# fp32r scores, a shared copy and a new compressed stage in the prompt attention of a Hawk/NSA decoder

## The chip, the cores and the metric

The kernel runs on one core of a Trainium2 chip. The metric is the device time of one execution in microseconds. Engines are called by their short names: PE (TensorE), PEld (its weight loads), DVE (VectorE), ACT (ScalarE), POOL (GpSimd), SP (SyncE, which only issues DMAs here). PA, PB and PCD are regions of PSUM: PA and PB of three banks each, PCD of two.

## The reference, cut to what matters

One inference step of a two-layer trunk for a prompt of 1024 tokens and 8 samples of one token: a Hawk layer (RG-LRU), then a layer of native sparse attention (NSA), each with a ConvFFN. The attention has 16 heads of 64 dimensions in four groups of four; the 4 heads of a group share keys and values. The part that the change touches:

```python
def nsa_attend(q_rot, q_raw, gates, q_pos, ctx, kw, vw, kw_pos):
    ...
    s_c = jnp.einsum('bcgrd,bngd->bcgrn', qr, ctx['kc']).astype(jnp.float32) * scale
    m_c = (ctx['cend'][None, :] <= q_pos[:, None])[None, :, None, None, :]
    p_c = masked_softmax(s_c, m_c)
    o_c = jnp.einsum('bcgrn,bngd->bcgrd', p_c, ctx['vc'].astype(jnp.float32))
    ...
    imp = jnp.einsum('bcgrn,nj->bcgj', p_c, ctx['cmp_to_sel'])
    ...
    top_val, top_idx = lax.top_k(imp, n_top)          # 8 of 16 blocks of 64 keys
    ...
    s_s = jnp.einsum('bcgrd,bcgkd->bcgrk', qs, k_g).astype(jnp.float32) * scale
    p_s = masked_softmax(s_s, m_s)
    o_s = jnp.einsum('bcgrk,bcgkd->bcgrd', p_s, v_g.astype(jnp.float32))
    ...
    s_w = jnp.einsum('bcgrd,bkgd->bcgrk', qs, kw).astype(jnp.float32) * scale
    p_w = masked_softmax(s_w, m_w)                    # window of 512 keys
```

`ctx['kc']` and `ctx['vc']` are 63 compressed keys and values per group, each made by a two-layer MLP with GELU from 32 tokens. q_rot and the keys of the selected and window branch carry a rotation of the first 16 dimensions of a head; the compressed branch uses q_raw.

## The kernel before

Stages follow one another: up to 1566 us the Hawk layer, its ConvFFN, keys and values and the q product; 1566 to 1693 us the compressed stage; 1693 to 2065 us the attention of the selected and the window branch; then the sample attention, the out projection and the second ConvFFN. Dense products are three fp32r products, high x high, high x low and low x high (tile(), L2051), of 128x128 weights with 348 columns; SP streams the weights, POOL splits them.

**Attention.** The prompt is cut in blocks (r, t, i): head r of its group, t = 0 or 1 the pair of groups (their two heads lie in the row halves 0 to 63 and 64 to 127, half = 0 or 1), i a tile of 128 queries. There are 64 blocks of two units (branch b = 0 selected, b = 1 window), each with the key tiles of 128 up to the diagonal: 528 tiles in all, cut in 152 groups of up to four tiles (112 of 4, 8 of 3, 24 of 2, 8 of 1). Neighbouring tiles of one branch form a run (runs()), one matmul for each half. Step s of PE is written out by hand in att_pe: transposes of group s-5 (L1232), scores of group s (L1219), values of group s-6 (L1243). Scores are plain f32 products into PA (half 0) and PB (half 1). DVE (att_dve) takes them with a custom operation that adds a mask, scales, writes to the ring in SBUF and keeps the minimum (L1302 for selected tiles, L1305 for diagonal and window tiles); behind each the accumulator is read and DVE is drained. Before each half of a group it writes one element (memset, L1294). It also inverts the sums of a unit (L1319) and adds the finished block to oc (L1313). ACT does the exponentials of a unit (L1275) and copies the transposed probabilities of each group from PCD to pt (copy_out, L1268). POOL multiplies the probabilities by gate and inverted sum (L1346, L1350). PE may write scores g when both maxima of group g-2 are done (max_done), transposes g when the copy of group g-1 is done (pt_ready).

**Compressed stage.** compress_pe makes the hidden layer of compressed keys, then values (L915), ACT the GELU (L998), PE the second layer (L950, L954), DVE copies. Then 16 blocks u = (t, i), i the query tile, eight heads at once: PE scores (L964), DVE mask, maximum and difference (shifted(), L1072 to L1078), ACT exponential, DVE sum, reciprocal and product (L1091 to L1098) and the importance of the 16 selection blocks (L1101 to L1108), POOL the gate (L1337), PE transpose (L979), ACT copy, PE product with vc (L991), ACT copy to oc. After every fourth block the eight largest of 16 are found (select_four, L1036 to L1048). The stage also works through modulation products for later (L284, L291, L315), whose weights SP loads. q is rotated on the way: its 16 leading dimensions of each head were packed through DRAM (pack_out, pack_in), DVE multiplies and adds 2064 columns in three steps at u = 4, 5, 6 (L1127 to L1131), and ACT's queue writes them back in place (turned_out, turned_back); the attention's first score waits for them (q_back).

## Time and profile before

| | us |
|---|---|
| three executions | 3223.52, 3218.14, 3211.95 |
| their median | 3218.14 |
| profiled execution | 3215.75 |
| its span in the profile | 3214.0 |
| busy PE / DVE / ACT / POOL in the span | 3083.8 / 1953.8 / 858.4 / 1186.4 |
| compressed stage (1566 to 1693) | 127 |
| selected and window attention (1693 to 2065) | 372 |

Busy is time in which an engine has an instruction under way; for PE the ends are modelled, so its busy time is an upper reading. What a stage waits for is read in that stage alone.

### The profile page before, as it was taken

The numbers are of one execution on the slowest core, as the hardware profiler recorded it, in microseconds if no ns is written. First come the engines' busy times: TensorE is split into PE (matmuls) and PEld (weight loads), VectorE is DVE, ScalarE is ACT, GpSimd is POOL, SyncE is SP. The second block draws the span as 40 slices with busy tenths as digits, with TensorE's granted clock in tenths as the row PEclk, the third lists the DMA queues.
The fourth block names the chain that finished last, engine by engine and source line by source line (L and its number), as shares of the span: only waits on it lengthen the run. The fifth ranks groups of instructions, "written<-read, shape, count | busy, mean of one in ns | idle before, by whom it ended". The sixth has DMA issues, their size and how long they took to land.

```text
span 3214.0 us, 56523 instructions
## 1 busy us (share of the span) xinstructions
PE 3083.8 (96%) x22530; PEld 2823.5 (88%) x22530; DVE 1953.8 (61%) x3639; ACT 858.4 (27%) x1337; POOL 1186.4 (37%) x801
## 2 busy tenths in 40 slices
PE   6999999999999999999989999998999999999996
PEld 4898989999999999899856666676989999999996
DVE  4567277566574756856377777402178558585676
ACT  4555131100010101302137888502131101010011
POOL 1332424434444443234115656301424444444441
PEclk8999999999999999999979999999999999999998
DMA  5222332121221212321455000185221111111112
GB/s 205 72 81 76 145 117 86 66 73 66 77 82 53 75 47 96 125 78 60 138 204 198 2 3 2 62 260 179 106 91 47 47 47 47 46 46 46 46 47 116
DMA packets 78015, 277.90 MB, mean 86 GB/s; under 512 B 8858, under 2 KB 19362, under 8 KB 74546
## 3 DMA queue, kind: packets, MB, share of 16 engines
q1 hardware_dynamic: 75202, 256.83, 23.5%
q10 hardware_dynamic: 2576, 17.73, 1.6%
q8 instruction: 171, 2.80, 0.4%
q14 instruction: 66, 0.54, 0.1%
HBM read 247.54 MB, written 36.27 MB: 88 GB/s over the span
## 4 chain that ended last, share of the span: by engine, by line
PE 78%; issue 6%; DVE 5%; SPq 3%; ACT 3%; DVEq 2%; DMA 1%; POOL 1%; POOLq 1%; ACTq 0%
PE PB L2051 32%; PE PA L2051 30%; PE PA L1219 2%; PE PCD L1232 2%; SPq L1648 1%; SPq L1649 1%; PE PB L1243 1%; PE PA L1243 1%; PE PA L2087 1%; PE PB L2087 1%; DVE ring L1305 1%; ACT ring L1275 1%; ACT pt L1268 1%; PE PCD L284 1%; DMA mw<-in_mw 1%
## 5 line engine op out<-in xcount | busy, mean ns | idle before, releaser
L1822 POOL TENSOR_TENSOR w_hi<-w_raw,misc 128x1024 fp32r<-128x1024 f32 x192 | 377.4, 1966 | 1504.2 <-PE PA L2051 624.5
L1824 POOL TENSOR_TENSOR w_lo<-w_raw,w_hi 128x1024 fp32r<-128x1024 f32 x192 | 560.0, 2917 | 27.3
L2051 PE MATMUL PA<-hB_hi,w_hi 128*128 128x348 f32 x1272 | 273.6, 323 | 0.0
L2051 PE MATMUL PB<-hB_hi,w_hi 128*128 128x348 f32 x1272 | 272.3, 322 | 0.0
L2051 PE MATMUL PB<-hB_hi,w_lo 128*128 128x348 f32 x1272 | 271.5, 322 | 0.0
L2051 PE MATMUL PA<-hB_hi,w_lo 128*128 128x348 f32 x1272 | 271.5, 322 | 0.0
L2051 PE MATMUL PB<-hB_lo,w_hi 128*128 128x348 f32 x1272 | 271.0, 321 | 0.0
L2051 PE MATMUL PA<-hB_lo,w_hi 128*128 128x348 f32 x1272 | 270.8, 321 | 0.0
L2051 PEld LDWEIGHTS PB<-hB_hi,w_hi 128*128 128x128 f32 x1272 | 214.9, 188 | 0.4
L2051 PEld LDWEIGHTS PB<-hB_lo,w_hi 128*128 128x128 f32 x1272 | 215.1, 188 | 0.0
L2051 PEld LDWEIGHTS PA<-hB_lo,w_hi 128*128 128x128 f32 x1272 | 215.0, 188 | 0.0
L2051 PEld LDWEIGHTS PA<-hB_hi,w_hi 128*128 128x128 f32 x1272 | 214.1, 188 | 0.4
L2051 PEld LDWEIGHTS PA<-hB_hi,w_lo 128*128 128x128 f32 x1272 | 214.2, 188 | 0.0
L2051 PEld LDWEIGHTS PB<-hB_hi,w_lo 128*128 128x128 f32 x1272 | 214.1, 188 | 0.0
L1350 POOL TENSOR_SCALAR ring<-ring,gtok,psm 128x640 f32<-128x640 f32 (+7 forms) x256 | 196.3, 771 | 0.1
L1275 ACT ACTIVATE ring<-ring,nmx 128x640 f32<-128x640 f32 (+7 forms) x256 | 185.1, 728 | 7.8 <-DVE nmx L1305 7.3
L486 DVE TENSOR_TENSOR ua<-ua,rms 128x1032 f32<-128x1032 f32 x48 | 111.9, 2330 | 67.8 <-ACT ua L424 67.5
L1268 ACT ACTIVATE pt<-PCD 128x1024 f32<-128x1024 f32 (+3 forms) x152 | 137.2, 903 | 51.0 <-PE PCD L1232 51.0
L486 DVE TENSOR_TENSOR ub<-ub,rms 128x1032 f32<-128x1032 f32 x46 | 85.4, 1856 | 85.7 <-ACT ub L424 85.7
L374 DVE TENSOR_TENSOR t<-t,sq 128x1032 f32<-128x1032 f32 x28 | 48.7, 1738 | 139.8 <-ACT sq L368 138.5
L537 DVE TENSOR_TENSOR O<-O,PB 128x1032 f32<-128x1032 f32 x40 | 49.1, 1228 | 134.2 <-PE PB L2051 133.3
L424 ACT ACTIVATE ua<-PA 128x1044 f32<-128x1044 f32 x24 | 25.1, 1045 | 392.1 <-PE PA L2051 390.3
(616 smaller groups left out, 6688.6 us busy)
## 6 DMA issues: line engine op xcount, KB each, us to landing
w_raw<-in_w SPq DMA_DIRECT2D x196, 512.0 KB, 3.6
mt<-in_mw SPq DMA_DIRECT2D x32, 1024.0 KB, 5.0
pages<-in_pages SPq DMA_DIRECT2D x64, 384.0 KB, 4.2
x_dram<-X SPq DMA_DIRECT2D x12, 1032.0 KB, 4.2
X<-x_dram SPq DMA_DIRECT2D x3, 4128.0 KB, 13.5
mw<-in_mw SPq DMA_DIRECT2D x4, 2048.0 KB, 23.1
mt_even<-in_mw SPq DMA_DIRECT2D x8, 1024.0 KB, 5.2
mt_odd<-in_mw SPq DMA_DIRECT2D x8, 1024.0 KB, 5.6
```

The costliest lines, as they stand in the source:

```text
L486: dve.tensor_tensor(u[:, 2:2 + TOK], u[:, 2:2 + TOK], rms, ALU.mult)
L537: dve.tensor_tensor(dst, dst, ps, ALU.add).then_inc(sem("sum_out"), 1)
L1219: mm = pe.matmul(PS[half][:, g % 2, n * P:(n + w) * P], QR[hs, r + 4 * t, i * P:(i + 1) * P], KH[b][hs, t, k * P:(k + w) * P], start=True, ...
L1232: mm = pe.transpose(PCD[e][:, c:c + 64], ring[half][q, x * P:(x + 1) * P], ident[q, q])
L1243: mm = pe.matmul(PS[j % 2][64 * half:64 * half + 64, 2, 0:P], VT[b][:, k, t * P + 64 * half:t * P + 64 * half + 64], flat(pt[g % 2])[:, (h ...
L1268: act.activation(to, of, ACT.Copy).then_inc(sem("pt_ready"), 1)
L1275: act.activation(p, p, ACT.Exp, bias=nmx[:, u % 16, half:half + 1], scale=-1.0, accum_out=psm[:, u % 16, half:half + 1]).then_inc(sem("exp ...
L1350: pool.tensor_scalar(p, p, gtok[:, i, gate:gate + 1], psm[:, u % 16, half:half + 1], ALU.mult, ALU.mult).then_inc(sem("p_ready"), 1)
L1822: pool.tensor_tensor(hi, raw, zero.broadcast_to([P, 1024]), ALU.add)
L1824: pool.tensor_tensor(lo, raw, hi.bitcast(F32), ALU.subtract).then_inc(sem("w_split"), 1)
L2051: mm = pe.matmul(PS[ps][:, c, 0:width], w[:, w0:w0 + P], x[:, k, c * width:(c + 1) * width], start=(k == 0 and n == 0), stop=(k == K - 1 a ...
L2087: mm = pe.matmul(PS[(p0 + b) % 2][:, c, 0:CW], w[(t + b) % 2][:, k * P:(k + 1) * P], x[:, k, c * CW:(c + 1) * CW], start=(first and i == 0 ...
```

## The change

Five things are changed.

1. The scores of the attention become three fp32r products each, q_hi x k_hi, q_hi x k_lo, q_lo x k_hi. ACT writes k_hi (k_high, six parts: four at the end of the compressed stage, two for t = 1 in the middle of the attention), POOL writes k_lo (k_low) and, for every block, q_hi and q_lo (q_parts). Blocks now run with t outermost.
2. The copy of the transposed probabilities of groups g with g % 3 == 2 goes from ACT to DVE, ahead of DVE's maxima of the same step. These are 50 of 152 groups: 38 of four tiles, 3 of three, 7 of two, 2 of one. The memset stays before the first half of a group only.
3. The last of the four selections moves into the attention (rank_four at step 10, drop_four at steps 12 and 14).
4. The compressed stage: compress v is cut in parts of 8, 4 and 4 products between other steps, the GELU is done for keys and values apart with each table loaded ahead, the DVE steps of block u+1 are interleaved with those of block u, the importance sum is two additions for the larger tiles, selections are spread over two or three blocks, and 48 products on idle PCD banks (IDLE_C) stand before PE's wait for POOL.
5. q is rotated for t = 0 in the Q stage and for t = 1 at u = 1 to 3, 1032 columns at a time. SP loads the rotation tables and the packed q between the last weight tiles of Q. The attention no longer waits for the rows to be written back (POOL waits for them, by half), but for q and k parts.

```diff
     def stage_c_pe(pe):
...
         for u in range(16):
...
+            if u >= 2:
+                pe.wait_ge(sem("oc_done"), u - 1)
+            warm(pe, PCD[u % 2], IDLE_C[u])
             pe.wait_ge(sem("pg_ready"), u + 1)
...
     def stage_c_dve(dve):
...
-            if u + 1 < 16:
-                shifted(u + 1)
+            if more:
+                masked(u + 1)
             dve.wait_ge(sem("ce_ready"), u + 1)
...
             dve.tensor_reduce(C["cs"], s3, AXX, ALU.add)
             dve.drain()
+            if more:
+                highest(u + 1)
...
             dve.reciprocal(C["cs"], C["cs"])
             dve.drain()
+            if more:
+                lowered(u + 1)
             dve.tensor_tensor(s3, s3, bn(C["cs"], i), ALU.mult).then_inc(sem("pc_done"), 1)
             dve.drain()
...
-            if i % 4 == 3:
-                select_four(dve, t, i - 3)
-            if 4 <= u <= 6:
-                rotate_dve(dve, u - 4)
+            if 1 <= u <= 3:
+                rotate_dve(dve, u - 1, 1)
+            if u in (3, 7, 11):
+                rank_four(dve, t, i - 3)
+            if u % 4 < 2 and u >= 4:
+                drop_four(dve, (u - 4) // QT, (u - 4) % QT // 4 * 4, u % 4)
...
-    BLOCKS = [(r, t, i) for r in range(4) for t in range(2) for i in range(QT)]
+    BLOCKS = [(r, t, i) for t in range(2) for r in range(4) for i in range(QT)]
...
+    def k_high(act, part):
+        t, b, c0, c1 = K_PARTS[part]
+        act.activation(KHI[t, b][:, c0:c1], KH[b][:, t, c0:c1], ACT.Copy).then_inc(sem("k_hi"), 1)
+
+    def k_low(pool, part):
+        t, b, c0, c1 = K_PARTS[part]
+        pool.wait_ge(sem("k_hi"), part + 1)
+        pool.tensor_tensor(KLO[b][:, t, c0:c1], KH[b][:, t, c0:c1], KHI[t, b][:, c0:c1].bitcast(F32),
+                           ALU.subtract).then_inc(sem("k_split"), 1)
+
+    def q_parts(pool, j):
...
+        q = QR[:, r + 4 * t, i * P:(i + 1) * P]
+        pool.tensor_tensor(qhi[j % 3], q, zero.broadcast_to([P, P]), ALU.add)
+        pool.drain()
+        pool.tensor_tensor(QLO[:, r + 4 * t, i * P:(i + 1) * P], q, qhi[j % 3].bitcast(F32), ALU.subtract).then_inc(sem("q_split"), 1)
...
     def att_pe(pe):
...
-        pe.wait_ge(sem("q_back"), 16 * 4)
+        pe.wait_ge(sem("qpk_turned1"), 16)
...
             for b, k, x, n, w in runs(g, False):
-                for half in range(2):
-                    hs = slice(64 * half, 64 * half + 64)
-                    mm = pe.matmul(PS[half][:, g % 2, n * P:(n + w) * P], QR[hs, r + 4 * t, i * P:(i + 1) * P],
-                                   KH[b][hs, t, k * P:(k + w) * P], start=True, stop=True, skip_group_check=True)
+                ks = slice(k * P, (k + w) * P)
+                for m, (q, kk) in enumerate(((q_hi, KHI[t, b]), (q_hi, KLO[b][:, t, :]), (q_lo, KHI[t, b]))):
+                    for half in range(2):
+                        hs = slice(64 * half, 64 * half + 64)
+                        mm = pe.matmul(PS[half][:, g % 2, n * P:(n + w) * P], q[hs], kk[hs, ks], start=(m == 0), stop=(m == 2),
+                                       skip_group_check=True)
...
+    def by_vector(g):
+        return g % 3 == 2
...
     def att_act(act):
...
-            if 0 <= s - LAG:
+            if 0 <= s - LAG and not by_vector(s - LAG):
                 copy_out(s - LAG)
...
     def att_dve(dve):
...
                 if half == 0:
                     after(dve, sem("t_done"), EVICTED[g])
-                dve.memset(dmark, 0.0)
+                    dve.memset(dmark, 0.0)
...
+        def copy_out(g):
+            dve.wait_ge(sem("t_done"), g + 1)
+            after(dve, sem("pv_done"), g - 1)
+            to, of = both_rows(g)
+            dve.tensor_copy(to, of).then_inc(sem("pt_ready"), 1)
...
         for s in range(NG + LAG + 2):
+            if 0 <= s - LAG < NG and by_vector(s - LAG):
+                copy_out(s - LAG)
...
+            if s == 10:
+                rank_four(dve, 1, 4)
+            if s in (12, 14):
+                drop_four(dve, 1, 4, (s - 12) // 2)
...
-        stream(T_KV + 8, T_O)
+        stream(T_KV + 8, T_Q + 5)
+        tables_in(sp)
+        stream(T_Q + 5, T_Q + 7)
+        pack_out(sp, 0)
+        tile_load(T_Q + 7, (T_Q + 7) % 2)
+        pack_in(sp, 0)
+        tile_load(T_Q + 8, (T_Q + 8) % 2)
```

On PE, one step in the middle of the attention. Before, scores of a selected run of four tiles, values of the group before, transposes of the next:

```order
L1219 MATMUL PA<-k_sel,xq 128x512 [waits max_done]
L1219 MATMUL PB<-k_sel,xq 128x512
L1243 MATMUL PA<-pt_154,v_sel 64x128 [waits pt_ready,oc_added]
L1243 MATMUL PA<-pt_154,v_sel 64x128
L1243 MATMUL PA<-pt_154,v_win 64x128 x2
L1232 MATMUL PCD<-ident,ring_163 128x64 [waits pt_ready,p_ready]
L1232 MATMUL PCD<-ident,ring_163 128x64 x7
L1232 MATMUL PCD<-ident,ring_164 128x64 x8
L1219 MATMUL PA<-k_sel,xq 128x128 [waits max_done]
```

After, at such a place (line 1322 scores, 1346 values, 1335 transposes):

```order
L1322 MATMUL PA<-k_hi_190,q_hi_196 128x512 [waits max_done]
L1322 MATMUL PB<-k_hi_190,q_hi_196 128x512
L1322 MATMUL PA<-k_lo_194,q_hi_196 128x512
L1322 MATMUL PB<-k_lo_194,q_hi_196 128x512
L1322 MATMUL PA<-k_hi_190,q_lo 128x512
L1322 MATMUL PB<-k_hi_190,q_lo 128x512
L1346 MATMUL PB<-pt_154,v_win 64x128 [waits pt_ready]
L1346 MATMUL PB<-pt_154,v_win 64x128
L1335 MATMUL PCD<-ident,ring_165 128x64 [waits pt_ready,p_ready]
L1335 MATMUL PCD<-ident,ring_165 128x64 x7
L1335 MATMUL PCD<-ident,ring_166 128x64 x8
L1322 MATMUL PA<-k_hi_189,q_hi_197 128x512 [waits max_done,q_split]
```

One f32 product for each half becomes three fp32r products for each half, in turns between PA and PB; the steps around it stand as before.

On DVE, the steps of one group in the attention. Before (1294 memset, 1302 mask and minimum, 1319 reciprocal):

```order
L1319 RECIPROCAL psm<-psm 128x2 [waits exp_done]
L1294 MEMSET misc 1x1 [waits t_done,s_done]
L1302 ISA ring_163,nmx<-PA,selm 128x512
L1302 ISA nmx 128x1
L1294 MEMSET misc 1x1
L1302 ISA ring_164,nmx<-PB,selm 128x512
L1302 ISA nmx 128x1
L1319 RECIPROCAL psm<-psm 128x2 [waits exp_done]
```

After (1404 memset, 1412 mask and minimum, 1423 the copy, 1437 reciprocal, 1429 the addition to oc):

```order
L1429 TENSOR_TENSOR oc<-oc,PA 128x128 [waits pv_done]
L1404 MEMSET misc 1x1 [waits t_done,s_done]
L1412 ISA ring_165,nmx<-PA,selm 128x512
L1412 ISA nmx 128x1
L1412 ISA ring_166,nmx<-PB,selm 128x512
L1412 ISA nmx 128x1
L1423 COPY pt_155<-PCD 128x2x6x64 [waits pv_done,t_done]
L1437 RECIPROCAL psm<-psm 128x2 [waits exp_done]
L1404 MEMSET misc 1x1 [waits t_done,s_done]
L1412 ISA ring_165,nmx<-PA,selm,nmx 128x384
```

The second memset is gone, and in every third step a copy from PCD stands ahead of the next group's maxima and ahead of the reciprocal, with waits for the transposes and for the values that read pt last.

On DVE, one block of the compressed stage. Before, shifted() of the next block (first four rows), then this block's sum to importance, then a rotation step of 2064 columns:

```order
L1072 TENSOR_TENSOR PA<-PA,cadd 128x8x9 [waits pg_ready,sc_done]
L1074 TENSOR_REDUCE cm<-PA 128x8
L1076 TENSOR_TENSOR pbuf_165<-PA,cm 128x8x56
L1078 MEMSET misc 1x1
L1091 TENSOR_REDUCE cs<-pbuf_166 128x8 [waits ce_ready]
L1096 RECIPROCAL cs<-cs 128x8
L1098 TENSOR_TENSOR pbuf_166<-pbuf_166,cs 128x8x48
L1101 TENSOR_REDUCE im_178<-pbuf_166 128x2x48
L1106 TENSOR_REDUCE im<-im_178 128x2x16
L1108 TENSOR_TENSOR im<-im,im_178 128x2x15
L1129 TENSOR_TENSOR qsw<-qsw,sinT 128x2064
```

After (1103, 1106 and 1112 belong to the next block, 1136 to 1172 to this one):

```order
L1103 TENSOR_TENSOR PA<-PA,cadd 128x8x9 [waits sc_done]
L1136 TENSOR_REDUCE cs<-pbuf_168 128x8 [waits ce_ready]
L1106 TENSOR_REDUCE cm<-PA 128x8
L1143 RECIPROCAL cs<-cs 128x8
L1112 TENSOR_TENSOR pbuf_167<-PA,cm 128x8x56 [waits pg_ready]
L1147 TENSOR_TENSOR pbuf_168<-pbuf_168,cs 128x8x48
L1116 MEMSET misc 1x1
L1162 TENSOR_TENSOR imt<-pbuf_168 128x4x48
L1164 TENSOR_TENSOR im_188<-imt 128x2x48
L1170 TENSOR_REDUCE im<-im_188 128x2x16
L1172 TENSOR_TENSOR im<-im,im_188 128x2x15
```

The next block's steps now stand between this block's, the difference is taken four steps later, and the importance takes one step more.

## Rows read from the trace of the kernel before

**Rows 1.** Busy us of PE, PEld, DVE, ACT, POOL by stage, clock, DMA share, GB/s.
```profile
1566.00:1693.00 127.00, 104.30 (x700) 71.19 (x699) 80.20 (x296) 38.08 (x72) 12.81 (x20) 0.77 0.66 207
1693.00:2065.00 372.00, 357.16 (x5027) 244.11 (x5028) 275.44 (x1490) 314.73 (x665) 218.12 (x384) 0.98 0.11 40
```

**Rows 2.** Waits in the attention, 1693 to 2065: us in total, times, longest us.
```profile
DVE psm L1319 <- ACT ring L1275: 21.2, 38, 3.3
PE PCD L1232 <- ACT pt L1268: 8.5, 19, 0.8
PEld PCD L1232 <- POOL ring L1350: 8.0, 25, 0.5
DVE ring L1305 <- PE PCD L1232: 7.9, 7, 1.1
DVE oc L1313 <- PE PB L1243: 5.9, 1, 5.9
```

**Rows 3.** Timeline of DVE, one half of a group: start us, duration us, line, operation.
```profile
1952.81 0.06 DVE L1294 MEMSET misc<- 1x1 f32 x1 [0.18 <-issue]
...
1953.54 0.08 DVE L1305 DVE_READ_ACCUMULATOR2_ANT nmx<- 128x1 f32 x1
1953.73 0.06 DVE L1294 MEMSET misc<- 1x1 f32 x1
```

**Rows 4.** Accumulator reads of the maxima by line: ns min/median/max, first, last start.
```profile
L1305 DVE DVE_READ_ACCUMULATOR2_ANT nmx<- x336: 81/83/85, 1694.4 to 2054.1; 128x1 f32 x168
...
L1302 DVE DVE_READ_ACCUMULATOR2_ANT nmx<- x160: 80/83/85, 1696.2 to 2050.0; 128x1 f32 x160
```

**Rows 5.** Timeline of PE, passes of two score runs: start us, duration us.
```profile
1886.79 0.65 PE L1219 MATMUL PA<-k_sel,xq 64*128 64x512 f32 x1
1886.79 0.65 PE L1219 MATMUL PB<-k_sel,xq 64*128 64x512 f32 x1
1887.28 0.59 PE L1219 MATMUL PA<-k_sel,xq 64*128 64x512 f32 x1
...
1889.57 0.48 PE L1219 MATMUL PA<-k_win,xq 64*128 64x384 f32 x1
...
1889.90 0.48 PE L1219 MATMUL PA<-k_win,xq 64*128 64x384 f32 x1
```

**Rows 6.** Chain that ended last, dense Q product: start us, us, count.
```profile
1531.60 11.49 PE PA L2051 x72
```

**Rows 7.** Groups by form, POOL, compressed stage: busy us, mean ns.
```profile
L1337 POOL TENSOR_TENSOR pbuf<-pbuf,gtok 128x128 f32<-128x128 f32 x2 | 0.8, 402 | 0.3
```

**Rows 8.** Copies: ACT's in the attention (busy us, mean ns), DVE's (ns min/median/max).
```profile
L1268 ACT ACTIVATE pt<-PCD 128x1024 f32<-128x1024 f32 x112 | 113.7, 1015 | 37.9 <-PE PCD L1232 37.9
...
L780 DVE COPY v_win<-PCD x4: 680/686/692, 1475.4 to 1485.2; 128x512 f32<-128x512 f32 x4
...
L2359 DVE TENSOR_TENSOR t<-O,PB x8: 1212/1220/1222, 3190.8 to 3207.1; 128x1024 f32<-128x1024 f32 x8
...
L773 DVE COPY k_win<-kb x2: 694/695/696, 1439.7 to 1453.2; 128x1024 f32<-128x1024 f32 x2
```

**Rows 9.** Timeline of DVE, compressed stage: selection's ends, a rotation, an importance sum.
```profile
1608.94 0.29 DVE L1036 TENSOR_TENSOR im<-im,m 128x128 f32<-128x128 f32 x1
...
1611.92 0.23 DVE L1072 TENSOR_TENSOR PA<-PA,cadd 128x72 f32<-128x72 f32 x1
...
1616.38 2.31 DVE L1127 TENSOR_TENSOR qpk<-qpk,cosT 128x2064 f32<-128x2064 f32 x1
...
1638.51 1.04 DVE L1101 TENSOR_REDUCE im<-pbuf 128x128 f32<-128x512 f32 x1
```

**Rows 10.** Compressed stage at 1636 to 1654: its window, and DVE behind it.
```profile
1636.00:1654.00 18.00, 18.00 (x80) 11.66 (x79) 11.60 (x59) 4.74 (x11) 2.62 (x5) 0.50 0.50 175
...
1650.74 0.23 DVE L315 TENSOR_TENSOR modT<-PB,vec 128x72 f32<-128x72 f32 x1 [3.97 <-PE PB L291]
```

**Rows 11.** Timeline of PE at the head of the compressed stage.
```profile
1585.40 0.44 PE L950 MATMUL PA<-hid,w 128*64 128x126 f32 x4 [1.56 <-ACT hid L998]
```

More of the change, by code:

```diff
@@ L896, in q_dve @@
             dve.tensor_tensor(q[:, NPR:TOK], q[:, NPR:TOK], q[:, TOK + 1:TOK + NC], ALU.add).then_inc(sem("q_scaled"), 1)
+            if n == 5:
+                for step in range(3):
+                    rotate_dve(dve, step, 0)
         dve.drain()
@@ L906, in q_dve, with compress_pe @@
         dve.drain()
-    def compress_pe(pe, k2, ps):
-        for kv in range(2):
-            out = ps[kv][:, 0:260].rearrange("p (g c) -> p g c", c=65)
-            for m in range(16):
-                mm = pe.matmul(out[:, :, 1:65] if m < 8 else out[:, :, 0:64], C["w1k" if kv == 0 else "w1v"][:, m, :],
-                               k2(kv, m % 8), start=(m == 0), stop=(m == 15), skip_group_check=True)
+    def compress_pe(pe, kv, first, last):
+        out = PB[:, kv, 0:260].rearrange("p (g c) -> p g c", c=65)
+        for m in range(first, last):
+            mm = pe.matmul(out[:, :, 1:65] if m < 8 else out[:, :, 0:64], C["w1k" if kv == 0 else "w1v"][:, m, :],
+                           K2[kv][:, m % 8, :, :], start=(m == 0), stop=(m == 15), skip_group_check=True)
         return mm
@@ L969, in stage_c_pe @@
         scores(1)
+        compress_pe(pe, 1, 12, 16).then_inc(sem("cmp_mm"), 1)
         pe.wait_ge(sem("gates_ready"), 1)
+        pe.wait_ge(sem("cmp_hidden"), 3)
+        for half in range(2):
+            for t in range(2):
+                mm = pe.matmul(PB[64 * half:64 * half + 63, 2, t * 64:(t + 1) * 64], C["hid"][:, 1, 2 * t + half, 0:63],
+                               C["w2"][:, 1, :], start=True, stop=True, skip_group_check=True)
+        mm.then_inc(sem("cmp_mm"), 1)
         for u in range(16):
@@ L1097, in stage_c_dve @@
             dve.drain()
+            if more:
+                lowered(u + 1)
             dve.tensor_tensor(s3, s3, bn(C["cs"], i), ALU.mult).then_inc(sem("pc_done"), 1)
             dve.drain()
-            dve.tensor_reduce(C["im0"][:, :, 0:seen(i)],
-                              pb[:, 0:512].rearrange("p (r h n) -> p h n r", r=4, h=2)[:, :, 0:seen(i), :], AXX, ALU.add)
+            if more:
+                scores_read()
+            if u == 0:
+                dve.wait_ge(sem("cmp_mm"), 6)
+                for half in range(2):
+                    vs = slice(64 * half, 64 * half + 63)
+                    cp = dve.tensor_copy(C["vc"][vs, :, 64 * half:64 * half + 64],
+                                         PB[vs, 2, 0:128].rearrange("p (t n) -> p t n", n=64))
+                cp.then_inc(sem("cmp_ready"), 1)
+            by_row = pb[:, 0:512].rearrange("p (r h n) -> p r h n", r=4, h=2)[:, :, :, 0:seen(i)]
+            if i >= 4:
+                two = C["imt"][:, :, :, 0:seen(i)]
+                dve.tensor_tensor(two, by_row[:, 0:2], by_row[:, 2:4], ALU.add)
+                dve.drain()
+                dve.tensor_tensor(C["im0"][:, :, 0:seen(i)], two[:, 0], two[:, 1], ALU.add)
+            else:
+                dve.tensor_reduce(C["im0"][:, :, 0:seen(i)], by_row.rearrange("p r h n -> p h n r"), AXX, ALU.add)
             dve.drain()
             q4 = C["im0"].rearrange("p h (j q) -> p h j q", q=4)
-            im = C["im"][:, :, i % 4, :]
+            im = C["im"][:, i // 4, :, i % 4, :]
             dve.tensor_reduce(im, q4, AXX, ALU.add)
@@ L1283, in att_act @@
                     exps(u)
+            for n in range(2):
+                if s == LAST_GROUP[16 + 4 * n]:
+                    act.wait_ge(sem("s_done"), LAST_GROUP[8 * n + 7] + 1)
+                    k_high(act, 4 + n)
         act.drain()
@@ L1338, in stage_c_pool @@
                                gtok[:, i, t * 8:t * 8 + 8].unsqueeze(2).broadcast_to([P, 8, seen(i)]), ALU.mult).then_inc(sem("pg_ready"), 1)
+            if u == 12:
+                k_low(pool, 0)
+            if u in (13, 14):
+                q_parts(pool, u - 13)
+        k_low(pool, 1)
+        k_low(pool, 2)
+        q_parts(pool, 2)
+        k_low(pool, 3)
     def att_pool(pool):
+        split = 3
         for u in range(NU):
@@ L1344, in att_pool @@
             n = len(branch_tiles(i, b)) * P
+            while split < len(BLOCKS) and FIRST_GROUP[split] - 5 <= UNIT_END[u]:
+                q_parts(pool, split)
+                split += 1
+            if u in (34, 42):
+                k_low(pool, 4 + (u - 34) // 8)
             pool.wait_ge(sem("sum_inverted"), u + 1)
@@ L1639, in smp_sp @@
         sp.wait_ge(sem("oc_done"), 16)
-        sp.wait_ge(sem("q_back"), 16 * 4)
+        for t in range(2):
+            sp.wait_ge(sem(f"q_back{t}"), 32)
         sp.dma_start(ptab, a["page_table"]).then_inc(sem("ptab_in"), 16)
```

209 lines of the change are left out of this document (126 added, 83 removed).

## The prediction

> **What bounds the kernel now.** I read the stage windows first, then inside each touched stage the waits and a stretch of each engine's instructions. The dense stages (0 to 1566 us and 2065 to 3214 us) are not changed in their arithmetic, and PE is busy through them. What moves the time lies in two stretches: the compressed stage, 127 us, and the attention of selected and window branch, 372 us [rows 1].
>
> In the attention PE is busy 357 us of the 372, DVE 275, ACT 315, POOL 218 [rows 1]. That looks like a PE-bound stage, and its waits agree: PE and its loads wait 8.5 us for ACT's copies and 8 us for POOL, with some 10 us in smaller pieces, so PE's own need is about 345 us [rows 2]. But DVE's 275 us is not its need. After each of the accumulator reads there is a gap of 0.11 us (a read of 0.08 us from 1953.54, the next start at 1953.73) in which nothing else can start, since the code drains there [rows 3]. There are 336 + 160 = 496 reads [rows 4]. So DVE is held 275.4 + 496 x 0.11 = 330 us of 372. Its idle time is 42 us: 21.2 us waiting for ACT's exponentials, 7.9 us for transposes that free a ring slot, 5.9 us once at the very end, and 7 us in small pieces [rows 2]. DVE has 42 us of room, PE 27.
>
> **Part 1: scores as three fp32r products.** Today a run of scores is taken by each of two row halves side by side in two passes. A 512-column pass starts 0.49 us after the one before (1886.79, 1887.28), a 384-column pass 0.33 us (1889.57, 1889.90), so 0.86 to 0.96 ns per column and pass [rows 5]. A full-height fp32r product of 348 columns takes 11.49 / 72 = 0.160 us, 0.458 ns per column [rows 6]. Three of those instead of two passes save 2 x 0.86 - 3 x 0.458 = 0.35 ns, at the upper spacing 0.54 ns, and over 528 tiles of 128 columns (67,584) 23 to 37 us of PE. That holds if the two 64-row halves of an fp32r product also run side by side, which no row shows; if they run one after the other, six of 0.458 ns instead of two of 0.86 to 0.96 cost 55 to 70 us more. I take the saving, by the f32 halves that start together, and use 23. PE's need becomes about 322 us.
>
> The parts themselves: k_hi is four ACT copies at the end of the compressed stage, k_lo and the q parts are POOL's. A POOL operation over 128 columns takes 0.40 us [rows 7]; 64 blocks x 2 = 51 us on an engine with 154 us idle in the attention [rows 1], issued blocks ahead. Cost at the end: none; if POOL were late, the scores of a block would wait some 0.8 us. At the start, PE no longer waits for the rotated rows to come back, but for four k parts; I count these as equal.
>
> **Part 2: every third copy on DVE.** 50 of 152 groups leave ACT: 38 of four tiles, 3 of three, 7 of two, 2 of one. ACT needs 1.015 us for four tiles [rows 8]. DVE's price from PSUM is 0.686 us for 512 columns, and for 1024 columns, one operand in PSUM, 1.220 us; between SBUF and SBUF 1024 take only 0.695 us [rows 8]. Ends of such records lie some 0.07 us past the next start, so I take 1.15, 0.9, 0.63 and 0.36 us: 38 x 1.15 + 3 x 0.9 + 7 x 0.63 + 2 x 0.36 = 51.5 us. These go on DVE, in front of the maxima of the same step. (The Trainium skill, "VectorE: DVE Perf Modes", section "Why PSUM operands drop a tier", says that a PSUM operand holds fp32 to one element per cycle, since PSUM has one read port for DVE. The rows agree: 0.686 us for half the columns that take 0.695 in SBUF. By the SBUF row the term would be 29 us.)
>
> The second memset of each group goes: 152 x 0.06 = -9 us [rows 3]. The last selection moves in from the compressed stage: +3 us (1608.94 to 1611.92) [rows 9].
>
> DVE's need: 330 + 51.5 - 9 + 3 = 375.5 us, which alone is more than the 372 us of the whole stage. The bound passes from PE to DVE, and PE's 23 us do not reach the end. To the need come what DVE can't fill: 11 us at the start and the end (1.2 us until the first scores are there, 3.3 us for the last exponentials, 5.9 us for the last values [rows 2]) and inner waits. The inner waits were about 30 us (42 less 11); ACT has 50 copies less to do, so its exponentials come sooner, but a DVE copy now waits for transposes too, and I keep half, 15. Attention: 375.5 + 11 + 15 = 401.5, so **+29.5 us**. Bounds: no inner waits at all and 1.06 us per copy, 383, so +11; all 30 us of inner waits left, 416.5, so +44.5.
>
> **Part 3: the compressed stage.** One of its 16 blocks is a chain on DVE: masks, maximum, difference, sum, reciprocal, product, importance, each drained. What goes:
> - rotation of q, 3 x 2.31 us over both halves of the heads: half is now done in the Q stage, beside PE's products [rows 6]: -3.5 us by the row of the first step [rows 9].
> - the fourth selection, to the attention: -3 us [rows 9].
> - the importance sum, 1.04 us at 512 columns [rows 9], becomes two additions of some 0.35 + 0.25 us plus one gap, for the eight blocks with the most columns: -1.4 us by that.
> - the next block's scores are interleaved with this one's reciprocal and product, so some 3 drains of about 0.07 us fewer per block: -3 us.
>
> Further, DVE waits for PE in this stage; the largest piece is 3.97 us at 1650.74, right behind a stretch in which the granted clock was 0.50 (the lower level, 1.2 GHz) and PE was busy all 18 us [rows 10]. PE had waited much in the blocks before. The change issues 48 extra products on idle banks ahead of its waits, and rotates earlier, so that these waits shorten; I count -6 us, between 0 and -10. (That the clock stays high with it is not shown by any row.) At the head, compress v is cut up so that PE has work while ACT does its GELU: PE waited 1.56 us there [rows 11] and 1 us for the copies behind, and each table load of 1.28 us moves ahead: -2.5 us, between 0 and -4.4. At its end a 2.4 us wait for the rotated rows goes, but four k_hi copies and k_lo products stand in its place: 0 to -2.4.
>
> The sum, -3.5 - 3 - 1.4 - 3 - 6 - 2.5 = -19.4, and the parts are not all on the chain at once; I take **-18 us**, bounds -6 and -22. The moves on SP's queue (rotation tables and packed q ahead of the last Q weight tiles) pass two weight loads of 512 KB; the tile before takes over ten microseconds of PE, and I count nothing; a late tile would cost 2 or 3 us. The sample stage's load that now waits for a group of the attention is needed only after 2065 us: nothing.
>
> **Sum.** The profiled execution took 3215.75 us, 2.4 us below the median of the three. 3215.75 + 29.5 - 18 = 3227.25, and with one microsecond for the risk at the weight loads **3228 us**.
>
> **The rivals.**
> - *Copies are cheap, faster.* If DVE copies at near its SBUF speed (29 us) and no inner wait is left, attention is 330 + 29 - 9 + 3 + 11 = 364, -8 us, and with -18 the whole comes to 3190. For it: ACT had the copies on PE's path (8.5 us of waits), and PE's need falls. Against it: the 512-column row. A chance of 0.15. (The Trainium skill, "TensorEngine Tiling (Array Packing)", section "PSUM Bottleneck", advises to use both ScalarE and VectorE for taking results out of PSUM once TensorE is faster. By it the change is right; here VectorE has 42 us of room and is asked for 51.5.)
> - *Near balance.* Need as computed, but the inner waits vanish: 386.5 us, 3215.75 + 14.5 - 18 = 3212. Chance 0.10.
> - *The compressed stage keeps its slow clock.* The extra products then lengthen PE's blocks and only the shorter DVE chain counts, -6: 3215.75 + 30 - 6 = 3240. Chance 0.13.
> - *The score halves do not run side by side, or narrow fp32r products cost like f32 ones.* PE's need becomes 345 + 55 to 70 = 400 to 415, both engines are at the bound and wait for each other: attention +40 to +58 with 12 to 15 us of waits, the whole 3238 to 3256. It decides from 400 us of PE. Chance 0.12. This and the forecast end slower.
> - Forecast: DVE becomes the attention's bound, 3220 to 3236. Chance 0.50.
>
> Faster and slower go by 0.3%, 9.65 us, about what a measurement of this kernel can tell from no change: below 3206 and above 3225. Faster: 0.15 and 0.02 of the near balance. Same: 0.08 of that, and the lowest third of the forecast's own case, 0.17: 0.25. Slower: 0.33 + 0.13 + 0.12 = 0.58. The range takes in the near balance, the forecast, the slow clock and the split halves: 3208 to 3256.
>
> **What would show it.** In the profile after: DVE held (busy plus reads x 0.11) over 92% of the attention, its waits for PE and ACT small, PE waiting for maxima (the line of the scores waits for nmx) for tens of microseconds, where it was 8 before; the copy on DVE at 1.15 to 1.25 us mean; a score run of 512 columns in 3 x 0.235 us with both halves at the same start. The compressed stage 105 to 121 us, its clock above 0.9. I would be wrong if the copies take 0.7 us, if PE still is the one not waiting, or if the dense stages move by over 3 us.

## The result and the profile after

The changed kernel takes 3236.29 us, median of 5 executions (3232.26 to 3242.31), the kernel before 3217.47 us in the same count; the ratio is 1.0059 with a 95% interval of 1.0048 to 1.0071. It is slower by 18.8 us; forecast were 3228 us and a range of 3208 to 3256.

The profiled execution of after took 3242.31 us, the longest of the five, with a span of 3240.5 us. Its stages (columns as in [rows 1]; the second row shows the attention, from the first score at 1686.39 to the last addition to oc at 2089.56):

```profile
1562.80:1686.40 123.60, 110.97 (x796) 79.58 (x795) 74.56 (x277) 40.83 (x78) 16.82 (x27) 0.82 0.58 174
1686.40:2090.00 403.60, 349.36 (x5426) 277.77 (x5427) 318.49 (x1414) 282.48 (x618) 277.89 (x512) 0.98 0.12 40
```

From the first product of the compressed stage (1563.28) to the first score are 123.1 us, before 126.4. The attention takes 403.2 us, before 371.3. The stages behind take 1150.9 us, before 1149.7, and the part ahead 3.3 us less; both lie within what these two parts differ by over all profiles below (the part ahead ended between 1561.8 and 1567.3). Over all profiles a small gain ahead is left: the part ahead is the same in the eleven kernels with the code of after there, and ended at 1564.4 us on the mean; in the three with the code of before it ended at 1567.0. So -3.3 - 3.3 + 31.9 + 1.2 = +26.5 us between the two spans, and nearly all is the attention.

There PE waits for a new releaser, the copy on DVE. Its idle time (the stretch less its busy time) rises from 372 - 357.2 = 14.8 us [rows 1] to 403.6 - 349.4 = 54.2 us. Of the waits in the attention after (us in total, times, longest us), against [rows 2]; a row of PE and one of PEld can cover the same moments, so the two don't add up to idle time of PE:

```profile
ACT pt L1374 <- PE PCD L1335: 96.0, 69, 3.0
POOL misc L1482 <- DVE psm L1437: 95.1, 61, 4.3
...
PE PCD L1335 <- DVE pt L1423: 31.1, 34, 2.1
PEld PCD L1335 <- POOL ring L1486: 28.8, 49, 2.1
ACT ring L1381 <- DVE nmx L1415: 23.8, 39, 2.0
...
PE PCD L1335 <- POOL ring L1486: 11.2, 18, 1.9
...
PE PA L1322 <- DVE nmx L1415: 7.6, 10, 2.2
```

The last row is the wait of the scores for the maxima, which the forecast had put at tens of microseconds: it stayed at 8. The late maxima show one step on, in ACT's 23.8 us of waits for them before its exponentials (5.5 us in g1, with the copies taken back). ACT, relieved of 50 copies, now waits 96 us for transposes: time it was given and can't use. The copies themselves, all four forms (busy us, mean ns), against [rows 8]:

```profile
L1423 DVE COPY pt<-PCD 128x1024 f32<-128x1024 f32 x38 | 46.5, 1224 | 9.5 <-issue 4.5 <-PE PCD L1335 4.4 <-PE PB L1346 0.3
...
L1423 DVE COPY pt<-PCD 128x512 f32<-128x512 f32 x7 | 4.8, 692 | 1.1 <-issue 1.1
...
L1423 DVE COPY pt<-PCD 128x768 f32<-128x768 f32 x3 | 2.9, 957 | 0.5 <-issue 0.5
...
L1423 DVE COPY pt<-PCD 128x256 f32<-128x256 f32 x2 | 0.8, 424 | 0.3 <-issue 0.3
```

That is 55.0 us of busy time and, with the 0.07 us by which each such record runs past the next start, the 51.5 us of the forecast. A score run of 512 columns in three fp32r products, from a timeline of PE (start us, duration us), against [rows 5]:

```profile
1949.99 0.48 PE L1322 MATMUL PA<-k_hi,q_hi 64*128 64x512 f32 x1
1950.02 0.47 PE L1322 MATMUL PB<-k_hi,q_hi 64*128 64x512 f32 x1
1950.31 0.40 PE L1322 MATMUL PA<-k_lo,q_hi 64*128 64x512 f32 x1
1950.34 0.39 PE L1322 MATMUL PB<-k_lo,q_hi 64*128 64x512 f32 x1
1950.55 0.39 PE L1322 MATMUL PA<-k_hi,q_lo 64*128 64x512 f32 x1
...
1950.89 0.44 PE L1346 MATMUL PA<-pt,v_sel 128*64 128x128 f32 x4
```

Both row halves start 0.03 us apart, so they do run side by side. The three products take 0.32, 0.24 and 0.34 us up to the values behind, 0.90 us in all; two f32 passes took 1.01 us, from the first start in [rows 5] to the values behind them. These two runs are typical: over the runs of this size that nothing held up, the median is 0.89 us in after (69 runs) and 1.01 us before (71 runs). In the kernel before, the values behind start here:

```profile
1887.80 0.44 PE L1243 MATMUL PA<-pt,v_sel 128*64 128x128 f32 x4
```

### The profile page after: what moved, and what is told of

It is laid out like the page before. It is cut to its first block, busy times and chain, and to the rows that moved or that the text cites. A ratio compares the mean times of both kernels' runs of the same rounds, so it can differ in the third digit from the quotient of the medians.

```text
span 3240.5 us, 57584 instructions
## 1 busy us (share of the span) xinstructions
PE 3079.2 (95%) x23026; PEld 2862.5 (88%) x23026; DVE 1998.6 (62%) x3548; ACT 828.6 (26%) x1295; POOL 1250.7 (39%) x935
## 4 chain that ended last, share of the span: by engine, by line
PE 72%; DVE 8%; issue 7%; SPq 3%; POOL 3%; DVEq 2%; ACT 2%; POOLq 1%; DMA 1%; ACTq 0%
PE PB L2189 32%; PE PA L2189 30%; DVE ring L1415 2%; POOL ring L1486 2%; SPq L1785 1%; SPq L1786 1%; PE PA L2225 1%; PE PB L2225 1%; DVE ring L1412 1%; PE PCD L291 1%; DMA mw<-in_mw 1%; DVEq L1416 1%; POOLq L1488 1%; PE PCD L1335 0%; PE PB L1577 0%
## 5 line engine op out<-in xcount | busy, mean ns | idle before, releaser
L1381 ACT ACTIVATE ring<-ring,nmx 128x640 f32<-128x640 f32 (+7 forms) x256 | 185.5, 727 | 24.8 <-DVE nmx L1415 23.8
L1335 PEld LDWEIGHTS PCD<-ident,ring 64*128 64x128 f32 x2112 | 80.0, 139 | 76.1 <-issue 47.3
L1335 PE MATMUL PCD<-ident,ring 64*128 64x64 f32 x2112 | 99.0, 230 | 45.8 <-DVE pt L1423 31.1
```

What stands on the lines that cost most here:

```text
L1335: mm = pe.transpose(PCD[e][:, c:c + 64], ring[half][q, x * P:(x + 1) * P], ident[q, q])
L1381: act.activation(p, p, ACT.Exp, bias=nmx[:, u % 16, half:half + 1], scale=-1.0, accum_out=psm[:, u % 16, half:half + 1]).then_inc(sem("exp ...
```

## The experiments

Theory A is the one of the prediction: the copies load DVE beyond what the stage holds. B, C and the later letters stand in the expectations. The table has the length of the compressed stage (first product to first score) and of the attention (first score to last addition) in each profiled execution, and the median time of all executions with its ratio to the kernel before, run on the same chip. Each length comes from one execution. In the attention that is enough: four kernels whose attention is the same (g1, h1, h2, i4) took 372.7 to 373.5 us. In the compressed stage it is not: the same code took 112.2 to 123.1 us.

| kernel | compressed | attention | median us | ratio, 95% |
|---|---|---|---|---|
| before | 126.4 | 371.3 | 3217.5 | |
| after | 123.1 | 403.2 | 3236.3 | 1.0059 (1.0048 to 1.0071) |
| g1_copies_act | 116.2 | 373.4 | 3203.5 | 0.9958 (0.9941 to 0.9974) |
| g2_before_copies | 126.3 | 405.4 | 3252.2 | 1.0116 (1.0100 to 1.0133) |
| g3_f32_scores | 123.1 | 404.6 | 3244.2 | 1.0082 (1.0063 to 1.0101) |
| g4_f32_act | 116.2 | 378.2 | 3207.1 | 0.9972 (0.9962 to 0.9982) |
| h1_reduce | 115.5 | 372.7 | 3200.7 | 0.9937 (0.9924 to 0.9951) |
| h2_no_idle | 112.4 | 373.5 | 3207.1 | 0.9964 (0.9950 to 0.9977) |
| h3_lag6 | 112.9 | 362.6 | 3193.9 | 0.9930 (0.9917 to 0.9944) |
| h4_no_q_parts | 112.8 | 375.0 | 3208.6 | 0.9971 (0.9961 to 0.9982) |
| i1_lag6_reduce | 113.4 | 362.3 | 3191.4 | 0.9915 (0.9902 to 0.9929) |
| i2_before_lag6 | 129.7 | 365.3 | 3212.1 | 0.9979 (0.9970 to 0.9989) |
| i3_every_sixth | 112.2 | 389.1 | 3220.8 | 1.0011 (1.0001 to 1.0020) |
| i4_late_gate | 120.3 | 372.9 | 3212.5 (one) | |

### The copies: taken back, and put into the kernel before

g1 takes the copies back in the changed kernel:

```diff
     def by_vector(g):
-        return g % 3 == 2
+        return False
```

> The changed kernel with all copies of transposed probabilities back on ACT; fp32r scores, parts, new compressed stage stay. Theory A (the copies made DVE the bound of the attention): DVE's need falls from about 375 to about 324 us, the attention, 403 us in the profile after, comes to 355 to 370 us, and the time to 3193 to 3208 us, below both kernels. Theory B (the parts of q and k on POOL delay the gated probabilities, for which PE waited 40 us after and 10 us before): the attention stays at 390 us or more and the time at 3225 us or more.

g2 is the kernel before with only this put in (and ACT skips these groups):

```diff
         for s in range(NG + LAG + 2):
+            if 0 <= s - LAG < NG and (s - LAG) % 3 == 2:
+                copy_out(s - LAG)
```

> The kernel before with one edit: the copy of every third group moves from ACT to DVE. Theory A: DVE's need rises from 330 to 381 us, and with the waits that stay the attention takes 400 to 410 us (371 before); the time is 3246 to 3258 us. Theory B: the attention stays within 10 us of 371 and the time below 3228 us.

Both times came out in the range of theory A, and so did g2's attention; g1's attention lies 3.4 us above its range. Without the copies the attention falls by 29.8 us, to 373.4, and the kernel is 0.42% faster than before instead of 0.59% slower. With them alone (and with both memsets kept) the attention of the old kernel rises by 34.1 us, to 405.4. PE's wait for DVE's copy has the same size there as in after:

```profile
PE PCD L1232 <- DVE pt L1319: 32.0, 38, 2.0
```

Theory B falls: the attention did not stay at 390 us in g1.

### How far DVE could take copies: every sixth

```diff
     def by_vector(g):
-        return g % 3 == 2
+        return g % 6 == 2
```

> The changed kernel with every sixth group's copy on DVE, 25 in place of 50 (g1 has none). DVE's need becomes 324 + 26 = 350 us. Theory A with the waits seen in g1 and after (DVE idles 30 us when it is the bound, about 50 us when not): attention 376 to 384 us, time 3208 to 3216 us. Rival (DVE has room for half the copies): attention 373 us as in g1, time 3203 us.

Both readings miss, A by 5 us. 25 copies cost 389.1 - 373.4 = 15.7 us, the next 25 cost 403.2 - 389.1 = 14.1 us. There is no point up to which DVE takes copies for nothing, though its idle time in g1 is still 373.4 - 269.6 - 54.6 = 49 us. Nor does a copy cost its full 1.1 us: about 0.6 us each, from the first. Each 25 copies add 24 or 25 us to DVE's busy time (269.6, 293.8, 318.5) and take 8 to 11 us from its idle time (49, 41, 30); the rest makes the stage longer. PE's waits for the copy say the same, 15.8 us here and 31.1 us with twice as many:

```profile
PE PCD L1335 <- DVE pt L1423: 15.8, 14, 2.1
```

A copy on DVE stands in order between maxima of two groups. PE needs both, in turn: the maxima of group g-2 to write scores g, the copy of group g-1 to write transposes g. Moved to DVE, the copy comes later by what DVE is at, and the maxima behind it later by the copy. That this order, and not the sum of DVE's work, sets the price is how I read the even slope; no run moved the copy to another place in the step.

### The scores: f32 again, with and without the copies on DVE

```diff
             for b, k, x, n, w in runs(g, False):
                 ks = slice(k * P, (k + w) * P)
+                if j < 63:
+                    for half in range(2):
+                        hs = slice(64 * half, 64 * half + 64)
+                        mm = pe.matmul(PS[half][:, g % 2, n * P:(n + w) * P], q_hi[hs].bitcast(F32),
+                                       KHI[t, b][hs, ks].bitcast(F32), start=True, stop=True, skip_group_check=True)
+                    continue
```

> The changed kernel with each score run of all blocks but the last as one f32 product of the high parts (the low parts are made as before but not used, so the result is coarser). Theory A: PE has room, so 15 to 20 us more PE work add at most 8 us: attention 403 to 411 us, time 3236 to 3244 us. Rival C (PE's own path sets the attention in the changed kernel too): the whole 15 to 20 us show, 3251 us or more.

> Both edits: f32 scores of the high parts and all copies on ACT (low parts made, not used). What is left of the change is the new compressed stage, the parts on ACT and POOL, the single memset and the new order of blocks. Theory A: the attention is near the 371 us of before, 363 to 373, and the fp32r products are worth what this kernel lies above the one with only the copies moved back, 8 to 18 us; time 3205 to 3218 us. Theory B: attention 390 us or more.

With the copies on DVE the f32 scores change the attention by 1.4 us (403.2 to 404.6), though PE is busy 10 us more (349.4 to 359.4): rival C falls for the attention. The median time, 3244.2, is just above the range given, and 7.9 us above after; the profile shows no more than 5 us of that, and I leave the rest open. With the copies on ACT the fp32r products are worth 378.2 - 373.4 = 4.8 us, 3.7 us by the medians, whose intervals overlap. That is under the 8 to 18 expected, and far under the 23 to 37 us of PE that the prediction gave them. PE's busy time in the two (attention, columns as before):

```profile
1680.00:2058.20 378.20, 354.43 (x5032) 243.33 (x5032) 270.34 (x1363) 316.71 (x668) 278.25 (x512) 0.99 0.13 42
```

```profile
1679.00:2052.40 373.40, 343.59 (x5424) 272.88 (x5424) 269.60 (x1363) 317.78 (x668) 278.54 (x512) 0.99 0.13 43
```

354.4 against 343.6: PE saves 10.8 us, not 23. Of these less than half reach the end: PE's idle time is 373.4 - 343.6 = 29.8 us in g1 and 23.8 us in g4. The waits that grow are those for POOL, in g1

```profile
PEld PCD L1335 <- POOL ring L1486: 26.5, 42, 1.7
...
PE PCD L1335 <- POOL ring L1486: 14.1, 21, 1.4
```

and in g4 (the rows of PE and PEld overlap, so their sums, 40.6 and 21.4 us, say which wait grew and not by how much PE stands longer):

```profile
PEld PCD L1341 <- POOL ring L1492: 15.5, 38, 1.3
...
PE PCD L1341 <- POOL ring L1492: 5.9, 12, 1.1
```

g4 shows one thing more. Its attention was expected at 363 to 373 us and took 378.2, 6.9 us more than before, though it has the f32 scores and the copies where they were. So the rest of the change (parts of k and q, the new order of blocks, the selection moved in, one memset less) lengthens the attention: 371.3 + 6.9 - 4.8 + 29.8 = 403.2. No run takes these pieces apart but for the q parts, which follow.

### POOL's parts and the distance to the transposes

h4 is g4 without q parts:

```diff
         q = QR[:, r + 4 * t, i * P:(i + 1) * P]
+        if j < 63:
+            pool.drain()
+            pool.tensor_tensor(pmark, zero[0:1], zero[0:1], ALU.add).then_inc(sem("q_split"), 1)
+            pool.drain()
+            return
...
-                        mm = pe.matmul(PS[half][:, g % 2, n * P:(n + w) * P], q_hi[hs].bitcast(F32),
+                        mm = pe.matmul(PS[half][:, g % 2, n * P:(n + w) * P], QR[hs, r + 4 * t, i * P:(i + 1) * P],
```

> As g4 (f32 scores, all copies on ACT), and scores read q itself, so that POOL makes no q parts but for the last block (k high parts alone are used, the result is coarser). Theory G: POOL loses 50 us, PE's waits for it fall to about the 10 us of before, and the attention from 378 to 366 to 371 us, time 3196 to 3203 us. Rival H: the attention stays at 375 to 380 us.

The attention is 3.2 us shorter in the profile, the median 1.5 us higher. The two rows of waits for POOL go from 21.4 to 15.3 us. So 53 us of q parts on POOL cost 0 to 3 us with f32 scores; 375.0 us is the lower end of what rival H gave. h3 keeps them and gives the chain more room:

```diff
-    LAG = 5
+    LAG = 6
```

> As g1, with transposes six groups behind the scores instead of five. Theory G (with the q parts on POOL the gated probabilities come late: PE waits 40 us for POOL in g1, 10 us before, and this eats what the fp32r scores save): with one more step of slack these waits fall under 15 us, the attention from 373 to 355 to 365 us, time 3190 to 3196 us. Rival H (POOL is only the last of several waits; DVE, held about 324 us plus its own waits, sets the pace): the attention stays at 368 us or more.

The attention falls by 10.8 us to 362.6, the time by 9.5 us, both as theory G has it. The waits for POOL fall from 26.5 and 14.1 us to 13.6 us of PEld and none of PE:

```profile
PE PCD L1335 <- ACT pt L1374: 14.0, 35, 0.8
...
DVE psm L1437 <- ACT ring L1381: 13.6, 26, 3.1
PEld PCD L1335 <- POOL ring L1486: 13.6, 41, 0.9
```

Is this the change's doing, or does the loop gain from it anyway? i2 is the same edit in the kernel before:

> The kernel before with transposes six groups behind the scores. Theory G (the sixth group pays since POOL makes the q parts now; before, PE waited only 10 us for POOL): 0 to -5 us, 3212 to 3218 us. Rival I (a sixth group of slack helps any version of this loop): the attention falls by 8 us or more, from 371 to 363 or less, time 3209 us or less.

It gains 6.0 us there (3218.07 to 3212.05, both of this comparison), and 6.0 in the attention, between what theory G (up to 5) and rival I (8 or more) gave. So 6 of h3's 10 to 11 us come from a slack that the loop lacked before already. The other 4 to 5 belong to the changed loop. That they come from its late probabilities fits the shorter waits for POOL, but is not shown by itself: no run had six groups of lag with f32 scores, or without q parts.

### The compressed stage: importance sum and idle products

```diff
-            if i >= 4:
+            if False:
                 two = C["imt"][:, :, :, 0:seen(i)]
```

> All copies on ACT (as g1, 3203.5 us) and the importance sum again as one reduction in place of two additions. In the profile after the first addition took 0.86 to 1.31 us, and ended each time some 0.1 to 0.2 us behind POOL's gate product that started beside it; the reductions of before took 0.71 to 1.05 us. Theory D (the additions cost time, not save it): the compressed stage is 2 to 4 us shorter at the same clock, time 3198 to 3202 us. Rival (they are beside the chain): no change, 3203.5.

DVE's busy time in the stage falls from 74.6 to 70.8 us, the stage from 116.2 to 115.5, the median by 2.8 us; the intervals of the two overlap. Theory D had asked for 2 to 4 us in the stage, so only its direction and the median bear it out. The first addition (busy us, mean ns; g1) and the reductions of the same blocks (h1):

```profile
L1162 DVE TENSOR_TENSOR imt<-pbuf 128x256 f32<-128x256 f32 x2 | 2.6, 1292 | 0.1
...
L1162 DVE TENSOR_TENSOR imt<-pbuf 128x160 f32<-128x160 f32 x2 | 1.7, 858 | 0.0
...
L1164 DVE TENSOR_TENSOR im<-imt 128x128 f32<-128x128 f32 x2 | 0.6, 294 | 0.1
```

```profile
L1166 DVE TENSOR_REDUCE im<-pbuf 128x128 f32<-128x512 f32 x2 | 2.1, 1049 | 0.1
...
L1166 DVE TENSOR_REDUCE im<-pbuf 128x80 f32<-128x320 f32 x2 | 1.4, 719 | 0.0
```

Why does an addition of 256 columns take 1.29 us? Each starts beside POOL's gate product, which the product ahead of it on DVE has released, and ends behind it. One such pair in after, 160 columns on DVE, 320 on POOL:

```profile
1608.47 0.72 POOL L1459 TENSOR_TENSOR pbuf<-pbuf,gtok 128x320 f32<-128x320 f32 x1 [6.07 <-DVE pbuf L1147]
```

```profile
1608.52 0.86 DVE L1162 TENSOR_TENSOR imt<-pbuf 128x160 f32<-128x160 f32 x1
```

i4 is g1 with POOL released after the additions instead, where there are additions:

```diff
-            dve.tensor_tensor(s3, s3, bn(C["cs"], i), ALU.mult).then_inc(sem("pc_done"), 1)
+            dve.tensor_tensor(s3, s3, bn(C["cs"], i), ALU.mult)
+            if i < 4:
+                dve.drain()
+                dve.memset(dmark, 0.0).then_inc(sem("pc_done"), 1)
...
-                dve.tensor_tensor(C["im0"][:, :, 0:seen(i)], two[:, 0], two[:, 1], ALU.add)
+                dve.tensor_tensor(C["im0"][:, :, 0:seen(i)], two[:, 0], two[:, 1], ALU.add).then_inc(sem("pc_done"), 1)
```

> As g1, but for i of 4 and more POOL is told to start its gate product only after the two importance additions. Theory D (an addition of two SBUF operands is held up by POOL's product beside it): the first addition takes 0.3 to 0.45 us for 160 to 256 columns, where it took 0.86 to 1.31. Rival (its access pattern is slow by itself): the same 0.86 to 1.31 us.

```profile
L1165 DVE TENSOR_TENSOR imt<-pbuf 128x256 f32<-128x256 f32 x2 | 0.9, 426 | 0.1
...
L1165 DVE TENSOR_TENSOR imt<-pbuf 128x160 f32<-128x160 f32 x2 | 0.7, 326 | 0.0
```

The same additions take 0.43 and 0.33 us: POOL beside them is what held them up. (The stage took 120.3 us in the one profile of i4, 116.2 in g1. POOL's product and what follows it start later there, but the same code of the stage differs by more than that between profiles, so nothing is shown by it.) The profile of after has the other case as well, a product of 384 columns on DVE that meets a k_lo part on POOL and takes 1.08 us, where it took 0.56 in the kernel before and 0.55 in after's other product of this size, with POOL idle (a row each of POOL and DVE after, then the one of before):

```profile
1665.04 1.26 POOL L1287 TENSOR_TENSOR k_lo<-k_win,k_hi 128x512 fp32r<-128x512 f32 x1 [6.03 <-ACT k_hi L1282]
```

```profile
1665.64 1.08 DVE L1147 TENSOR_TENSOR pbuf<-pbuf,cs 128x384 f32<-128x384 f32 x1
```

```profile
1623.09 0.56 DVE L1098 TENSOR_TENSOR pbuf<-pbuf,cs 128x384 f32<-128x384 f32 x1
```

(The Trainium skill, "SBUF — State Buffer", section "SBUF: two separate sides", says that a DVE operation with two SBUF inputs and a POOL operation that reads SBUF lock each other out for a whole instruction. The traces agree: 1.29 us beside POOL, 0.43 us alone. A reduction has one input; in h1 each of the eight largest started within 0.05 us of POOL's product and ended within 0.05 us of it, after 1.05 us for 512 columns, so it ran beside it and did not wait for its end.)

h2 is g1 with the idle products left out:

```diff
-    IDLE_C = (4, 0, 0, 0, 12, 3, 0, 2, 8, 0, 0, 0, 12, 3, 2, 2)
+    IDLE_C = (0,) * 16
```

> As g1, without the 48 extra products on idle banks. Theory E (they keep the clock up in some stretches, but lie in PE's own chain where the clock is low: 16 of them took 3.75 us from 1637.62 at block 8): the compressed stage changes by less than 5 us in all, 113 to 120 us. Rival F (they hold the clock and are what the new stage gains): without them the compressed stage takes 122 us or more, time 3210 us or more.

The compressed stage of its profile is the shortest but one, 112.4 us, at a granted clock of 0.89, the median is 3.6 us above g1 and the intervals overlap: 48 products neither help nor hurt beyond what can be measured. The profiled execution was the fastest of h2's five, 3198.5 us against a median of 3207.1, so its stage may be shorter than is usual. Rival F is out for the profile; a loss of up to 4 us in the median stays possible.

### Both together

> All copies on ACT, transposes six groups behind, importance sum as one reduction: the sum of h3 and h1. If what they gain adds, 2 to 4 us less than h3's 3193.9, so 3188 to 3192 us; attention 360 to 365 us. If the reduction's gain is lost in the clock's course through the compressed stage, 3194 us.

i1 takes 3191.4 us, 0.85% less than before (0.71 to 0.98) and 1.4% less than after: the best kernel of the study. It is 2.6 us below h3, as h1 is 2.8 below g1; twice the same small gain, each within the intervals, so the reduction's part is likely and not shown.

## Why the prediction was right, and where it was not

**Result.** Direction and range held; +18.8 us against +12. Too small a gain in the compressed stage (the step that failed, below) made the difference; the attention came out within 2 us, in part by luck.

**DVE's need in the attention: right.** Forecast 375.5 us; measured 318.5 + 496 x 0.11 = 373.1 us. Its idle time, forecast as 11 + 15, is 30.1 us. The attention: 401.5 forecast, 403.2 measured, +31.9 against +29.5. That "DVE becomes the attention's bound" as the cause of the slowdown is borne out by g1 and g2, which move it by 30 and 34 us with the copies alone. "The bound passes from PE to DVE, and PE's 23 us do not reach the end": g3 confirms the second half, 1.4 us. The first half is too simple. If a bound had passed, the first 25 copies would have cost less than the next; i3 shows 15.7 and 14.1 us. The 42 us of room that I gave DVE [rows 2] are not room: more than half of a copy's time shows from the first one. A need plus waits that stay is no model for this loop either: DVE's idle time is 49, 41 and 30 us with 0, 25 and 50 copies. That it was near the 26 us of the sum at 50 copies, and that the 6.9 us of the rest of the change (g4) were not in the sum at all, is why I call the close number luck in part.

**The signs.** Of those that were named, four came: DVE held 373.1 of 403.2 us, 92.5%; its waits for ACT's exponentials 5.1 us in all, 21.2 before [rows 2]; the copy at 1.224 us; both halves at one start. PE's wait for maxima, said to grow from 8 to tens of microseconds, did not grow (7.6 us); PE waits 31.1 us for the copy itself, which must be done before its next transposes. The compressed stage, said to take 105 to 121 us at a clock above 0.9, took 123.1 at 0.82 in this profile, 112.2 to 116.2 at 0.90 to 0.94 in five others. And the part ahead moved by 3.3 us, just over the 3 that were to count against the forecast, which did not foresee it.

**fp32r products: the mechanism right, the term mis-sized.** The halves run side by side, as taken. I multiplied a full-height rate, 0.458 ns a column [rows 6], with all columns. Only the middle one of three products comes near it (0.24 us for 512, where 0.458 ns a column makes 0.235; the others take 0.32 and 0.34), and the run as a whole saves 0.11 us of 1.01, and PE 10.8 us instead of 23 (g4 against g1). Since PE's saving did not reach the end here, the error was covered; with the copies on ACT it shows, 4.8 us in the attention.

**Parts on POOL at no cost: nearly right.** h4 against g4: 0 to 3 us for the q parts, which keep POOL busy 53 us in after (51 forecast). But with faster scores the waits for POOL are longer, as g1 against g4 shows.

**Compressed stage: direction right, size wrong.** The step that failed was the sum of -18. The pair of profiles shows -3.3 us. Seven profiles of kernels with the stage of after all but unchanged (after, g1, g3, g4, h3, h4, i3) took 123.1, 116.2, 123.1, 116.2, 112.9, 112.8 and 112.2, mean 116.7; three with the stage of before 126.4, 126.3 and 129.7, mean 127.5. So the change is worth about -10.8 us, inside the bounds of -6 and -22, and the profiled execution of after was at the slow end; its stage is 6.4 us longer than that mean, and it lies 6 us above its median. With the means of all four parts the sum closes: -2.5 ahead, -10.8, +31.9 and -0.6 behind make +18.0 us, measured +18.8. By terms:
- The head, forecast -2.5: the first transposes come 24.4 us after the stage's start instead of 27.8, -3.4.
- DVE's work, forecast -10.9, of which 7.9 would show as busy time: busy 80.2 to 74.6, -5.6. The importance sum, forecast -1.4, is +3.8 by h1. I priced the additions by their columns and did not ask what runs on POOL beside them. What the 3 us of drains came to, no run shows.
- Waits for PE at the low clock, forecast -6, which no row had shown: in the profiled pair DVE's waits for this PE line (the folds of the modulation products) rose from 8.4 to 18.6 us instead. The granted clock of the stage went from 0.77 to 0.82 in the profiled pair, and was 0.90 to 0.94 in five of the other six. In after it is low again where the forecast had it rise:

```profile
1620.00:1641.00 21.00, 18.81 (x89) 13.47 (x89) 11.53 (x48) 4.24 (x9) 2.80 (x4) 0.53 0.55 169
1587.00:1594.00 7.00, 6.28 (x30) 3.65 (x31) 4.74 (x16) 1.83 (x4) 1.45 (x4) 0.50 0.32 102
```

```profile
1637.62 3.75 PE L385 MATMUL PCD<-ident 128*128 128x128 f32 x16
```

```profile
1643.60 0.23 DVE L322 TENSOR_TENSOR modT<-PB,vec 128x72 f32<-128x72 f32 x1 [10.20 <-PE PB L298]
```

Here eight of the extra products (16 records, two for each f32 product) took 3.75 us at the low clock, in PE's own chain, and DVE then waited 10.2 us for PE, where the longest such wait was 4.0 us before [rows 10]. h3, the same code up to here, had the full clock from 1587 to 1594 and took 10.2 us less for the stage:

```profile
1587.00:1594.00 7.00, 5.08 (x52) 3.03 (x50) 5.92 (x23) 2.73 (x6) 1.74 (x4) 1.00 0.49 176
```

What makes one execution take the one course and another the other is not settled: the parts ahead of the stage are the same, and the stage starts 1.4 us apart. The extra products don't seem to decide it: h2 has none, and its stage had a clock of 0.89.

**The rivals.** Copies at SBUF speed are excluded by their own time, 1.224 us for four tiles, and these and near balance by g1 and g2. The split halves are excluded by the starts. The slow clock held in part, in some executions. (The Trainium skill, "TensorEngine Tiling (Array Packing)", section "PSUM Bottleneck", which advises to use both ScalarE and VectorE, speaks of a case in which the PSUM copy has become the bottleneck. It was none here: ACT's copies kept PE 8.5 us waiting [rows 2], and once a third of them was DVE's, those kept it 31.1.)

## What to carry to other kernels

Before work is moved to an engine with idle time, ask who waits for that engine in every step: idle time in a loop whose engines release each other in turn is no room, and a third of the copies on DVE cost 0.6 us each of 1.1, from the first. When one engine of such a loop gets faster, lengthen the distance between its steps: one more group of lag was worth 10 us here with the change (copies on ACT) and 6 us without it; the faster scores alone brought 5. And judge a stage whose clock falls and rises by several profiles: one pair showed -3.3 us here, ten profiles -10.8. Last, price a DVE operation with two SBUF inputs by what POOL does at that moment.

## What was not expected of the hardware

An addition of 256 columns from SBUF took 0.43 us alone and 1.29 us beside a POOL product of 1.04 us. The same code of the compressed stage took 112.2 to 123.1 us, with a mean granted clock of 0.94 in the shortest and 0.82 in the longest. A 64-row fp32r product of 512 columns took 0.24 us behind another and 0.32 us behind the transposes.
